# Half-size products for the MLP down projections of groups 1 to 6

## The reference, cut to what matters

```python
def squared_relu_mlp(h, w_up, w_down):          # w_up 1024 x 4096, w_down 4096 x 1024
    return jnp.square(jax.nn.relu(h @ w_up)) @ w_down
...
        x = x + rms_norm(o, norm_g[i, 1])
        h = rms_norm(x, norm_g[i, 2])
        x = x + rms_norm(squared_relu_mlp(h, mlp_w_up[i], mlp_w_down[i]), norm_g[i, 3])
```

## Time and profile before

| | us |
|---|---|
| median of 3 runs | 2551.8 (2550.17 to 2553.77) |
| span of the profiled execution | 2548.7 |
| PE busy in it | 2494.2 (98%) |
| PEld busy | 2362.4 (93%) |
| DVE busy | 918.6 (36%) |
| ACT busy | 836.6 (33%) |
| POOL busy | 542.8 (21%) |

### The profile page before, as it was taken

One profiled execution on the slowest core, in us unless ns is written; L12 is line 12 of the kernel. 1 busy time (PEld: TensorE's weight loads), 2 busy tenths in 40 slices (PEclk: granted clock), 3 DMA queues, 4 the chain that ended last, 5 costly groups with the idle time before them and its releaser, 6 DMA issues.

```text
span 2548.7 us, 41743 instructions
## 1 busy us (share of the span) xinstructions
PE 2494.2 (98%) x17518; PEld 2362.4 (93%) x17518; DVE 918.6 (36%) x1813; ACT 836.6 (33%) x1658; POOL 542.8 (21%) x304
## 2 busy tenths in 40 slices
PE   8999999999999999999999999999999999999998
PEld 8888887799999999999999877699999999999997
DVE  6555445427221221222238344507322222222226
ACT  5554545446111121121136455627220120121112
POOL 0101011134121121121126110115211212212213
PEclk9999999999999999999999999999999999999999
DMA  3101101124111111111115100114111111111114
GB/s 110 46 21 43 35 24 41 34 86 135 50 42 41 49 41 41 43 47 41 53 34 162 55 26 18 30 34 157 63 43 42 42 48 41 41 49 41 41 60 130
DMA packets 62720, 138.98 MB, mean 55 GB/s; under 512 B 8544, under 2 KB 39520, under 8 KB 62592
## 3 DMA queue, kind: packets, MB, share of 16 engines
q1 hardware_dynamic: 54720, 130.51, 16.0%
q10 hardware_dynamic: 7808, 6.56, 0.9%
q0 software_dynamic: 64, 0.10, 0.0%
HBM read 117.74 MB, written 19.40 MB: 54 GB/s over the span
## 4 chain that ended last, share of the span: by engine, by line
PE 88%; DVE 5%; ACT 3%; issue 2%; DMA 0%; ACTq 0%; SPq 0%; POOL 0%; DVEq 0%; POOLq 0%
PE banks L223 53%; PE banks L203 21%; PE banks L1942 4%; PE banks L2077 1%; PE banks L2096 1%; DVE y L650 1%; DVE norm_acc_x L610 1%; PE banks L1452 1%; PE banks L1433 1%; PE banks L1420 1%; PE banks L1460 1%; PE banks L2086 1%; ACT banks L522 1%; DVE norm_acc L599 1%; PE banks L2061 0%
## 5 line engine op out<-in xcount | busy, mean ns | idle before, releaser
L166 POOL TENSOR_TENSOR w_lo<-w_raw,w_hi 128x1024 fp32r<-128x1024 f32 x164 | 404.4, 2470 | 1835.9 <-ACT w_hi L159 1835.9
L203 PE MATMUL banks<-h_hi,w_hi 128*128 128x384 f32 (+1 forms) x1224 | 423.3, 346 | 4.4 <-DVE h_lo L2507 1.8
L203 PE MATMUL banks<-h_lo,w_hi 128*128 128x384 f32 (+1 forms) x1224 | 404.6, 331 | 0.0
L203 PE MATMUL banks<-h_hi,w_lo 128*128 128x384 f32 (+1 forms) x1224 | 404.3, 330 | 0.0
L159 ACT CAST w_hi<-w_raw 128x1024 fp32r<-128x1024 f32 x180 | 187.1, 1046 | 464.9 <-DMA w_raw<-in_units 464.8
L223 PE MATMUL banks<-h_hi,w_hi 128*128 128x384 f32 (+1 forms) x1368 | 301.8, 329 | 0.0
L223 PE MATMUL banks<-h_lo,w_hi 128*128 128x384 f32 (+1 forms) x1368 | 301.3, 328 | 0.0
L223 PE MATMUL banks<-h_hi,w_lo 128*128 128x384 f32 (+1 forms) x1368 | 301.3, 328 | 0.0
L223 PE MATMUL banks<-mlp_a_hi,w_hi 128*128 128x384 f32 (+1 forms) x1344 | 297.6, 330 | 1.5 <-issue 1.3
L223 PE MATMUL banks<-mlp_a_lo,w_hi 128*128 128x384 f32 (+1 forms) x1344 | 296.1, 328 | 0.0
L223 PE MATMUL banks<-mlp_a_hi,w_lo 128*128 128x384 f32 (+1 forms) x1344 | 296.0, 328 | 0.0
(11 more groups left out here) (205 smaller groups left out, 3183.0 us busy)
## 6 DMA issues: line engine op xcount, KB each, us to landing
w_raw<-in_units SPq DMA_DIRECT2D x180, 512.0 KB, 3.5
x_scratch<-y SPq DMA_DIRECT2D x48, 192.0 KB, 2.8
norm_x<-x_scratch SPq DMA_DIRECT2D x28, 192.0 KB, 3.2
x_scratch<-y SPq DMA_DIRECT2D x24, 160.0 KB, 1.9
norm_x<-x_scratch SPq DMA_DIRECT2D x20, 160.0 KB, 3.0
y<-in_x SPq DMA_DIRECT2D x16, 192.0 KB, 5.2
out_y<-y SPq DMA_DIRECT2D x16, 192.0 KB, 3.3
norm_x<-in_x SPq DMA_DIRECT2D x12, 192.0 KB, 3.3
```

The lines of the kernel that those rows point to most:

```text
L166: c.nc.gpsimd.tensor_tensor(c.w_lo[:, s], c.w_raw[:, s], c.w_hi[:, s].bitcast(F32), ALU.subtract).then_inc(self.ready, 1)
L203: mm = chip.nc.tensor.matmul(out, w, x, start=(first and n == 0), stop=(last and n == 2))
```

## The change

For groups 1 to 6 of both MLPs, the down projection of a group is a product of a 1024 x 512 and a 512 x 1088 matrix. The change cuts both into two by two quadrants (output tiles 0 to 3 and 4 to 7, even and odd hidden tiles, first and second half of the tokens, `HALF_T` = 544) and computes them with seven quadrant products in place of eight, by the scheme of Strassen and Winograd:

- Output tiles p and p + 4 make pair p, four pairs a group. For a pair, SP loads one unit with its four weight quarters (128 x 256 each) into one slot; `mix` on DVE writes the four combinations of quarters that are needed into a second slot, by three chained subtractions (512, 256 and 256 columns). ACT rounds three quarters of the first slot and all of the second, POOL subtracts both. A pair so holds two of the four slots; a group loads four up units and four pair units, eight as before.
- On the data side, DVE makes four sums a pair of hidden tiles (`add`, 544 columns each, eight a group), ACT rounds and DVE subtracts fourteen parts of 544 columns a group, in place of four tiles of 1088.
- PE makes each of the seven products in 2 (tiles) x 3 (passes) x 2 (halves of 272 columns) = 12 matmuls, so 84 a pair and 336 a group. Each uses two PSUM banks, a slot of four. Three of the seven (i = 2, 5, 6) accumulate on top of an earlier product (i = 0, 1, 3) that stays in its banks, and begin only when DVE has read that one (`slot_free`).
- DVE adds each of the 28 products of a group into a quadrant of `y` (`take_product`, 544 columns), in order. `mix` of pair p + 1 stands in DVE's list between takes 1 and 2 of pair p; that of pair 0 is in the up stage. `y` is held in another basis during groups 1 to 6, so that one addition a product is enough; `change_basis` (two subtractions of 4 x 544 columns) runs before group 1 and before group 7.
- The order on PE becomes: up tiles 1, 2, 3 of group g, up tile 0 of group g + 1, then the products of group g. In group 7 PE waits ahead of up tile 1 until all products have been added, and ACT issues the first loads of x for the closing normalisation only when tile 0's low part is done.
- Raw hidden values lie where `a_lo` (or `s_lo`) will be; semaphores are shared by both MLPs. Group 0, the last wave, the GLA stage and the SWA stage keep their instructions.

The core of the diff (T is 1088, KT 8, P 128, UNIT 1024):

```diff
+HALF_T = T // 2
+QUARTER = 2 * P
+PAIRED = range(1, FF_GROUPS - 1)
+PAIRS = 4
...
+            for n in range(FF_TILES):
+                s = (n + 1) % SLOTS
+                sp.wait_ge(self.used, 12 * g + (before + n - SLOTS + 1))
+                sp.dma_start(self.chip.w_raw[:, s], self.units[8 * g + (first + n)]).then_inc(self.raw_in[s], 16)
+            for p in range(PAIRS):
+                s = self.pair_slots(p)[0]
+                sp.wait_ge(self.used, 12 * g + (before + FF_TILES + 2 * p - SLOTS + 1))
+                sp.dma_start(self.chip.w_raw[:, s], self.units[8 * g + (first + FF_TILES + p)]).then_inc(self.raw_in[s], 16)
...
+    def mix(self, dve, u0, p, g):
+        (s, t), n = self.pair_slots(p), 3 * self.pair_number(u0, p, g)
+        nc, raw, to = self.chip.nc, self.chip.w_raw[:, s], self.chip.w_raw[:, t]
+        of = lambda x, i: x[:, i * QUARTER:(i + 1) * QUARTER]
+        dve.wait_ge(self.raw_in[s], 16 * self.pair_raw_count(u0, p, g))
+        dve.wait_ge(self.used, 12 * g + (self.group_slots_before(u0) + FF_TILES + 2 * p + 1 - SLOTS + 1))
+        two = lambda x: x.rearrange("p (j n) -> p j n", j=2)
+        nc.vector.tensor_tensor(two(to[:, 0:2 * QUARTER]), of(raw, 0)[:, None, :].to_broadcast([P, 2, QUARTER]),
+                                two(raw[:, QUARTER:3 * QUARTER]), ALU.subtract).then_inc(self.mixed, 1)
+        dve.wait_ge(self.mixed, n + 1)
+        nc.vector.tensor_tensor(of(to, 2), of(raw, 2), of(to, 0), ALU.subtract).then_inc(self.mixed, 1)
+        dve.wait_ge(self.mixed, n + 2)
+        nc.vector.tensor_tensor(of(to, 3), of(to, 2), of(raw, 3), ALU.subtract).then_inc(self.mixed, 1)
+    def high_pair(self, act, u0, p, g):
+        (s, t), nc, c = self.pair_slots(p), self.chip.nc, self.chip
+        act.wait_ge(self.raw_in[s], 16 * self.pair_raw_count(u0, p, g))
+        nc.scalar.copy(c.w_hi[:, s, QUARTER:UNIT], c.w_raw[:, s, QUARTER:UNIT]).then_inc(self.pair_hi, 1)
+        act.wait_ge(self.mixed, 3 * self.pair_number(u0, p, g) + 3)
+        nc.scalar.copy(c.w_hi[:, t], c.w_raw[:, t]).then_inc(self.pair_hi, 1)
...
+    def low_pair(self, pool, u0, p, g):
+        n, c = 2 * self.pair_number(u0, p, g), self.chip
+        pool.wait_ge(self.mixed, 3 * self.pair_number(u0, p, g) + 3)
+        for i, (s, at) in enumerate(zip(self.pair_slots(p), (slice(QUARTER, UNIT), slice(0, UNIT)))):
+            pool.wait_ge(self.pair_hi, n + i + 1)
+            c.nc.gpsimd.tensor_tensor(c.w_lo[:, s, at], c.w_raw[:, s, at], c.w_hi[:, s, at].bitcast(F32),
+                                      ALU.subtract).then_inc(self.pair_ready, 1)
...
+    PRODUCTS = (Product(A11, 1, 0, False), Product(S3, 5, 1, False), Product(A12, 3, 0, True), Product(S1, 4, 2, False),
+                Product(S2, 6, 3, False), Product(S4, 2, 1, True), Product(A22, 7, 2, True))
+    N_PROD = len(PRODUCTS)
...
+        def product(p, i, kappa):
+            prod = self.PRODUCTS[i]
+            s, at = ws.pair_slots(p)[prod.block // 4], prod.block % 4 * QUARTER + kappa * P
+            w_hi, w_lo = (w[:, s, at:at + P] for w in (chip.w_hi, chip.w_lo))
+            x_hi = self.part(prod.part, kappa, self.a_hi, self.s_hi)
+            x_lo = self.part(prod.part, kappa, self.a_lo, self.s_lo)
+            half, bank = HALF_T // 2, self.SLOT_BANKS[prod.slot]
+            for n, (w, x) in enumerate(((w_hi, x_hi), (w_hi, x_lo), (w_lo, x_hi))):
+                for c in range(2):
+                    mm = nc.tensor.matmul(chip.banks[:, bank + c, 0:half], w, x[:, c * half:(c + 1) * half],
+                                          start=(not prod.adds and kappa == 0 and n == 0), stop=(kappa == 1 and n == 2),
+                                          skip_group_check=True)
+                    if n == 0 and c == 0:
+                        ws.tell_used(mm)
+            if kappa == 1:
...
+        def slot_free(g, p, i):
+            added = self.READS * g + (self.adds + self.N_PROD * p)
+            if i in (0, 1, 3):
+                if p == 0:
+                    pe.wait_ge(self.up_taken, FF_TILES * g + (self.ups + (4 if i < 2 else 5)))
+                else:
+                    pe.wait_ge(self.prod_added, added + {0: 3, 1: 6, 3: 7}[i] - self.N_PROD)
+            elif i in (2, 5, 6):
+                pe.wait_ge(self.prod_added, added + {2: 1, 5: 2, 6: 4}[i])
...
+        def paired_down(g):
+            for p in range(PAIRS):
+                for i in range(self.N_PROD):
+                    if i < 2:
+                        ws.wait_pair(pe, u0, p, g, i)
+                    slot_free(g, p, i)
+                    for kappa in range(2):
+                        if p == 0:
+                            a_ready(g, i, kappa)
+                        product(p, i, kappa)
+                    if i >= self.N_PROD - 2:
+                        ws.finish()
...
+        with pe.Fori(PAIRED.start, PAIRED.stop) as g:
+            for j in range(1, FF_TILES):
+                up(g, j)
+            up(g + 1, 0)
+            paired_down(g)
...
+        def take_product(g, p, i):
+            first, second, upper = slice(0, HALF_T), slice(HALF_T, T), p + KT // 2
+            m, cols = {2: (p, first), 5: (upper, first), 6: (p, second)}.get(i, (upper, second))
+            n = self.N_PROD * p + i
+            dve.wait_ge(self.prod_full, self.READS * g + (self.prods + n + 1))
+            dve.wait_ge(self.prod_added, self.READS * g + (self.adds + n))
+            y = chip.y[:, m, cols].rearrange("p (c n) -> p c n", c=2)
+            nc.vector.tensor_tensor(y, self.slot_banks(self.PRODUCTS[i].slot), y, ALU.add).then_inc(self.prod_added, 1)
...
+        def change_basis():
+            upper, lower = slice(KT // 2, KT), slice(0, KT // 2)
+            first, second = slice(0, HALF_T), slice(HALF_T, T)
+            for m, cols in ((upper, first), (lower, second)):
+                y = chip.y[:, m, cols]
+                nc.vector.tensor_tensor(y, chip.y[:, upper, second], y, ALU.subtract).then_inc(self.turned, 1)
...
+        take_up(PAIRED.start, 0, self.t_raw[:], self.SET_BANKS[1])
+        with dve.Fori(PAIRED.start, PAIRED.stop) as g:
+            for kappa in range(2):
+                if kappa:
+                    take_up(g, 2, self.t_raw[:], self.SET_BANKS[1])
+                add(g, kappa, self.S3)
+                low(g, kappa, self.A11)
+                low(g, kappa, self.S3)
+                if kappa:
+                    ws.mix(dve, u0, 0, g)
+                take_up(g, 2 * kappa + 1, self.a_raw[:, 2 * kappa + 1], self.SET_BANKS[0])
+                for part in (self.S1, self.S2, self.S4):
+                    add(g, kappa, part)
+                for part in (self.A12, self.S1, self.S2, self.S4, self.A22):
+                    low(g, kappa, part)
+            take_up(g + 1, 0, self.t_raw[:], self.SET_BANKS[1])
+            for p in range(PAIRS):
+                for i in range(self.N_PROD):
+                    if i == 2 and p < PAIRS - 1:
+                        ws.mix(dve, u0, p + 1, g)
+                    take_product(g, p, i)
```

More of the change, by code:

```diff
@@ L152, in load_rounds, with load_groups @@
                 sp.dma_start(self.chip.w_raw[:, s], self.units[SLOTS * i + s]).then_inc(self.raw_in[s], 16)
[L154 to L158 removed]
+    def load_groups(self, sp, u0):
+        self.load_rounds(sp, u0 // SLOTS + 1, u0 // SLOTS + 2)
+        self.load(sp, u0 + 8)
+        before, first = self.group_slots_before(u0), u0 + 9 - 8 * PAIRED.start
+        with sp.Fori(PAIRED.start, PAIRED.stop) as g:
+            for n in range(FF_TILES):
[6 more added lines that the diff above has]
+                sp.dma_start(self.chip.w_raw[:, s], self.units[8 * g + (first + FF_TILES + p)]).then_inc(self.raw_in[s], 16)
+        for unit in range(u0 + 8 * PAIRED.stop + 1, u0 + MLP_UNITS):
+            self.load(sp, unit)
@@ L1164, in vector @@
+        dve.wait_ge(self.turned, self.turns + 4)
         for b in range(NB):
```

421 lines of the change are left out of this document (276 added, 145 removed).

## The result

The changed kernel takes 2477.93 us (median of 4 runs, 2476.98 to 2480.0) beside 2552.03 us for the kernel before on the same chip: a ratio of 0.971, 95% interval 0.9697 to 0.9724. The forecast was 2481, range 2472 to 2508. The profiled execution has a span of 2475.2 us where that of before had 2548.7: 73.5 us less.

What follows compares the result with a forecast made beforehand. The prediction took a full TensorE, matmul count times pace, as the bound: 2548.7 - 72.5 (products) + 2.0 (edges) = 2478.2 us of span, and with the median 3.1 us above it 2481 us, range 2472 to 2508.

Steps and rivals of the forecast that it cites:

- What bounds the kernel: Groups 1 to 6 of both MLPs: PE never waits, so time is matmul count times pace; a group is 96.21 us.
- Step 1: PE's products: 336 matmuls at 125.5 ns, 42.2 us, replace 48.0 us a group; 72.5 us less over twelve groups.
- the line through 256 and 320 columns: Estimate of PE's pace at 272 columns from the paces at two neighbouring widths: 124.8 ns a matmul.
- the slower stretch of 72 matmuls: 72 matmuls of 256 columns at 119.9 ns, scaled to 127.4 ns at 272 columns as the upper pace.
- The width plus a tenth: PE's matmul pace: a tenth above a column a cycle at 2.4 GHz, not a fixed charge a matmul.
- Step 2: DVE between products: takes of 0.72 us and `mix` of some 1.6 us come in time; PE is not held up.
- Step 3: Weights of the next pair: loaded, mixed, rounded and subtracted before PE needs them, 2 to 3 us to spare.
- Step 4: Hidden values on DVE: the added work makes 47 us of 90 a group, covered by up tiles; nothing on the path.
- Step 5: Edges: in group 7 up tile 1 waits 1.0 us for the last take, twice, +2.0 us; `change_basis` is covered.
- The rival of the shared port: `mix` steps meeting POOL subtractions stand 0.87 us longer, making takes late: 27 us more, 2508 us; chance 13%.
- The rival of the weight loads: A load's turn on PE of 166.7 ns whatever the width makes a group 104.0 us, the time 2647 us; chance 5%.
- The rest of the sum: Whole kernel: the median lies 3.1 us above the profiled span, taking 2478.2 us to 2481 us.

Runs made afterwards that it cites:

- e2_eighth: Changed kernel with product i = 4 made twice in every pair, so eight products a pair as before; 2551.67 us, ratio 0.9998 to the kernel before.
- e5_mix_at4: Changed kernel with `mix` moved from behind take 1 to behind take 3 in DVE's list; 2519.03 us, ratio 0.9872 to the kernel before.
- e4_edge: Changed kernel with group 7's up tiles using the banks in the other order, so up tile 1 waits only for the last take but one; 2477.06 us.
- e7_two_sbuf: Changed kernel plus two unused 512-column DVE additions with two SBUF inputs behind take 2 of every pair; 2623.55 us, ratio 1.0278 to the kernel before.
- 384 + 160: Changed kernel with each product, and its take, cut into 384 + 160 columns in place of 272 + 272; 2552.22 us, ratio 1.0 to the kernel before.

## Why the prediction was right, step by step

- **What bounds the kernel.** Right. PE is full before and after, and the chain is PE for group after group. `e2_eighth` shows it from the other side: the same number of columns, the same time.
- **Step 1, the pace.** The term was 42.2 us a group for 336 matmuls at 125.5 ns, and measured 41.94 at 124.8, which is the lower of its two bounds, the line through 256 and 320 columns. I should have taken that bound: the slower stretch of 72 matmuls was the worse neighbour. With it a group is 89.93 us and not 90.17. These 0.24 us, 12 times, are 2.9 of the 3.0 us by which the predicted span (2478.2) missed 2475.2. "The width plus a tenth" was right for 272 columns, but the prediction gave it as the whole rule, and the uneven divisions show that it is not: below some 236 columns the load's turn of 108 ns is the pace.
- **Step 2, DVE between products.** Right. The take was put at 0.72 us and has a mean of 724 ns; `mix` was to end at 5.6 us of the pair and ended at 5.4. The slack it left before product 6, close to 2 us, is bracketed by the `mix` done twice (free) and three times (36 stops).
- **Step 3, the weights.** Right. Pair 1's low parts were to be ready 9.8 us into pair 0: POOL's block of two from 839.34 ends at 843.55, 9.8 us after 833.78. How near the limit lies is seen in `e5_mix_at4`: 3 us later, PE waits on `w_lo`.
- **Step 4, the hidden values.** Right: 47 us of DVE a group were counted, 46.08 are there, and no wait on them appears in groups 1 to 6.
- **Step 5, the edges.** Right: 1.0 us each predicted, 0.99 and 0.99 measured, named as predicted, and the wait is gone in `e4_edge`.
- **The rival of the shared port.** The mechanism is real and larger than it was priced: up to 2.1 us a step and not 0.87. It doesn't strike because of where `mix` stands, which was the argument against it; `e7_two_sbuf` shows a place where it would have turned the change into a loss.
- **The rival of the weight loads.** The mechanism is real too, below some 236 columns, and its price was wrong: 166.7 ns was the pace of another width, not a load's turn. At 108 ns it stands 17 ns below the pace of 272 columns and 35 below the 143.0 ns at which the change would be worth nothing. That break-even was right: 384 + 160 has a mean of 142.7 ns (47.95 / 336) and comes out level with the kernel before.
- **The rest of the sum.** The profiled span lies 2.7 us below the median, where 3.1 were added. No two errors cancel in the sum: the products were 0.23 us a group too long, the edges within 0.01 us, and this last term 0.4 us too long.

## What to carry to other kernels

When one engine is full and the chain is nothing else, price a change by that engine's instruction count times a pace read from starts at the neighbouring widths, and check that no piece is narrower than the turn of its weight load. Work that is moved to another engine is free until its slack is used up, and then costs nearly in full (1.44 us a stop for a third `mix` of 1.63); find the slack by counting due times, and look in each pair or phase, also in those that don't have the moved work. Put a DVE operation on SBUF data where GpSimd is idle, since the price is up to the other's whole instruction.

## What was not expected of the hardware

- A 128x128 weight load has a turn of some 108 ns (106 and 109 from two divisions), though its record lasts 0.19 us; a matmul of 32 columns and one of 160 add the same to a stream of loads and matmuls. A load of 64 columns has a turn of some 55 ns.
- DVE operations with two SBUF inputs, and a TENSOR_SCALAR with one (426 ns for 512 columns at its least), stood up to 2.1 us behind a GpSimd subtraction. The other way round it happens as well: GpSimd's 1024-column subtraction, 2404 ns at the median, reached 4653 in the changed kernel:
```profile
L219 POOL TENSOR_TENSOR w_lo<-w_raw,w_hi x116: 2355/2404/4653, 79.5 to 2413.9; 128x1024 fp32r<-128x1024 f32 x116
```
  The longest of them stands under `change_basis` behind the first MLP's last products (timeline of the changed kernel):
```profile
1236.33 4.76 DVE L1416 TENSOR_TENSOR y<-y 128x2176 f32<-128x2176 f32 x2
1241.01 3.50 DVE L1453 TENSOR_TENSOR mlp_a_lo<-mlp_late_t_raw,mlp_a_hi 128x1088 fp32r<-128x1088 f32 x1
...
1238.71 8.07 POOL L219 TENSOR_TENSOR w_lo<-w_raw,w_hi 128x1024 fp32r<-128x1024 f32 x2 [5.79 <-ACT w_hi L214]
```
  POOL starts during the second of the long DVE instructions (done at 1241.09), and its first instruction takes 4.65 us, the 4653 of the row above; DVE's next one, 1088 columns that take 1292 ns at the mean of the earlier trace rows, takes 3.50. The two engines alternate, each standing until the other's instruction is over. All of it lies under an up tile and costs nothing.
- Why a matmul at a granted clock of 1.00 takes a tenth more than a column a cycle (117.4 ns at 256 columns, 124.8 at 272, 166.7 mean for 384 + 384 + 320) was not settled by any run here and stays open.
